# Feed-forward chunks in groups of 3, 6, 6, 7 instead of 4, 6, 6, 6, with the operand splits moved, in a two-layer encoder step

## The reference

```python
def swiglu(h, w_gate, w_up, w_down):
    return (jax.nn.silu(h @ w_gate) * (h @ w_up)) @ w_down
...
    for layer in range(DEPTH):
        x = x + 0.5 * swiglu(rms_norm(x, norm_g[layer, 0]), ffn_w_gate[layer, 0], ffn_w_up[layer, 0], ffn_w_down[layer, 0])
        h = rms_norm(x, norm_g[layer, 1])
        ...
        x = x + 0.5 * swiglu(rms_norm(x, norm_g[layer, 2]), ffn_w_gate[layer, 1], ffn_w_up[layer, 1], ffn_w_down[layer, 1])
    return (rms_norm(x, final_norm_g), ...)
```

## Time and profile before

| | us |
|---|---|
| runs (3) | 1987.78, 1988.15, 1989.62; median 1988.15 |
| the profiled execution, its own time | 1988.24 |
| its span, first to last instruction | 1986.4 |
| PE busy | 1978.6 in 13462 matmuls |
| DVE, ACT, POOL busy | 1418.2, 932.5, 964.0 |
| mean granted TensorE clock | 0.999 of full speed |

### The profile page before, as it was taken

One profiled execution on the slowest core, in us unless ns is written; L12 is line 12 of the kernel. 1 busy time (PEld: TensorE's weight loads), 2 busy tenths in 40 slices (PEclk: granted clock), 3 DMA queues, 4 the chain that ended last, 5 costly groups with the idle time before them and its releaser, 6 DMA issues. The chain is left out here.

```text
span 1986.4 us, 35197 instructions
## 1 busy us (share of the span) xinstructions
PE 1978.6 (100%) x13462; PEld 1957.5 (99%) x13462; DVE 1418.2 (71%) x2263; ACT 932.5 (47%) x1642; POOL 964.0 (49%) x1043
## 2 busy tenths in 40 slices
PE   9999999999999999999999999999999999999998
PEld 8999999999999999999999999999999999999998
DVE  5778687664766667878766668778767866878665
ACT  6354454543434435445455345454545535455443
POOL 2556666632000055676663336666743355666643
PEclk9999999999999999999999999999999999999999
DMA  6232324323222223232432222323332223232412
GB/s 162 74 86 70 101 70 117 101 58 95 66 64 65 56 73 86 77 95 69 117 102 75 64 65 75 96 80 91 102 109 70 67 57 86 77 99 65 122 38 86
DMA packets 312853, 165.28 MB, mean 83 GB/s; under 512 B 15539, under 2 KB 310271, under 8 KB 312688
## 3 DMA queue, kind: packets, MB, share of 16 engines
q1 hardware_dynamic: 307840, 157.31, 28.4%
q0 software_dynamic: 2672, 4.65, 1.0%
q10 hardware_dynamic: 2176, 1.07, 0.2%
HBM read 159.01 MB, written 4.00 MB: 82 GB/s over the span
## 5 line engine op out<-in xcount | busy, mean ns | idle before, releaser
L2401 POOL TENSOR_TENSOR sums<-in_raw,sums 128x256 f32<-128x256 f32 (+1 forms) x416 | 440.1, 1088 | 12.1 <-DVE in_lo L1751 3.9
L2401 POOL TENSOR_TENSOR sums<-in_raw 128x256 f32<-128x256 f32 (+1 forms) x208 | 179.9, 885 | 429.7 <-DVE in_lo L1751 377.4
L895 PE MATMUL psum<-xg_hi,in_lo 128*128 128x320 f32 x1152 | 356.0, 309 | 0.0
L893 PE MATMUL psum<-xg_hi,in_hi 128*128 128x320 f32 x1152 | 355.9, 309 | 0.0
L894 PE MATMUL psum<-xg_lo,in_hi 128*128 128x320 f32 x1152 | 355.9, 309 | 0.0
L1751 DVE TENSOR_TENSOR in_lo<-in_raw,in_hi 128x1024 fp32r<-128x1024 f32 (+1 forms) x208 | 271.9, 1309 | 42.5 <-ACT in_hi L1306 42.2
L893 PE MATMUL psum<-mix_hi,in_hi 128*128 128x320 f32 x864 | 267.0, 309 | 0.0
L894 PE MATMUL psum<-mix_lo,in_hi 128*128 128x320 f32 x864 | 267.0, 309 | 0.0
L895 PE MATMUL psum<-mix_hi,in_lo 128*128 128x320 f32 x864 | 267.0, 309 | 0.0
L1306 ACT ACTIVATE in_hi<-in_raw 128x1024 fp32r<-128x1024 f32 (+1 forms) x208 | 205.0, 991 | 111.7 <-PE psum L895 111.7
L744 PE MATMUL psum<-xg_hi,in_hi 128*128 128x320 f32 x800 | 252.3, 315 | 0.9 <-DVE in_lo L1792 0.6
(11 more groups left out here) (267 smaller groups left out, 4560.9 us busy)
## 6 DMA issues: line engine op xcount, KB each, us to landing
in_raw<-in_ffn_w_gate SPq DMA_DIRECT2D x87, 512.0 KB, 5.2
in_raw<-in_ffn_w_up SPq DMA_DIRECT2D x86, 512.0 KB, 4.0
in_raw<-in_ffn_w_down SPq DMA_DIRECT2D x64, 384.0 KB, 4.0
out_raw<-in_ffn_w_down SPq DMA_DIRECT2D x32, 384.0 KB, 3.5
out_raw<-in_ffn_w_down SPq DMA_DIRECT2D x32, 256.0 KB, 2.9
in_raw<-in_mix_w_in SPq DMA_DIRECT2D x14, 512.0 KB, 4.6
out<-y_nat SPq DMA_DIRECT2D x5, 512.0 KB, 3.1
in_raw<-in_mix_w_in SPq DMA_DIRECT2D x8, 256.0 KB, 4.5
```

The source lines that it names most:

```text
L893: pe.matmul(dst, w_hi[:, k], v_hi, start=k == 0 and slot in (0, 1, 4), stop=False, skip_group_check=True)
L895: end = pe.matmul(dst, w_lo[:, k], v_hi, start=False, stop=k == wide - 1, skip_group_check=True)
L2401: last = pool.tensor_tensor(to[:, part], a[:, part], b[:, part], op)
```

## The change

One chunk per FFN goes from the plain group to the last group, whose outputs then have 7 chunks; `PLAIN` is 3 and `FAST` 19. Around that:

- The plain units are (0,0), (1,0), (0,1), (1,1), (2,0), (2,1) (chunk, half): six instead of eight. The first outputs wait for the third chunk's hidden rows only at that chunk.
- The first outputs have 9 matmuls a unit instead of 12, the last ones 21 instead of 18. Their PSUM banks are turned by one in the last group, since the last step now has the other parity.
- The seven blocks of x are split in another order and place: before T3 and T2 during the plain chunks, B11 and B21, T1, T4 and B22 in the first outputs; now B11, B21 and T1 there, one at a time, and T2, B22, T3 and T4 in the first seven-product step. Parts 3 and 4 of the first step's weights move into that step too.
- The seventh hidden row of the last group has its own place over the weights' sums (`last_hi`, `last_lo`), so its split waits for the last step's weight splits. The last group's upper products use `pair_even`, which lies over the sums of squares `ss`; these are now cleared after that group's hidden rows and not at its first step.

The diff, cut to its core:

```diff
-GROUPS = (4, 6, 6, 6)
+GROUPS = (3, 6, 6, 7)
...
+def ends(fast):
+
+    return fast % FAST in (5, 11, 18)
...
+        last_hi = over("last_hi", [P, TOKENS], arena + 30720, F32R)
+        last_lo = over("last_lo", [P, TOKENS], arena + 33280, F32R)
...
+        def out_bank(g, i, q):
+
+            return 4 + (q + (g == 3)) % out_banks(g, i)
...
-            return (pair_even, pair_odd)[i % 2][:, :] if g in SEVEN else t2a[:, :]
+            return (pair_even, pair_odd)[i % 2][:, :] if g in SEVEN else pair_even[:, :]
...
-        BLOCKS = ["T3", "T2", "B11", "B21", "T1", "T4", "B22"]
+        BLOCKS = ["B11", "B21", "T1", "T2", "B22", "T3", "T4"]
...
                             def before_k(k):
                                 if g == 0 and i == 0 and j == 0 and k == 0:
-                                    pe.wait_ge(hidden_lo, 44 * index + 2 * gk - (2 if half == 0 else 0))
+                                    pe.wait_ge(hidden_lo, 44 * index + 2 * (gk - 1))
+                                if g == 0 and i == 0 and j == 0 and k == gk - 1:
+                                    pe.wait_ge(hidden_lo, 44 * index + 2 * gk - (1 if half == 0 else 0))
...
             def blocks_between(index, phase, i, q):
 
                 if (i, q) == (0, 3):
-                    act.wait_ge(in_mm, IN_UNIT[phase] + 8)
+                    act.wait_ge(in_mm, IN_UNIT[phase] + 2 * PLAIN)
                     block_split("B11")
+                elif (i, q) == (1, 1):
                     block_split("B21")
-                elif (i, q) == (1, 1):
+                elif (i, q) == (1, 3):
+                    act.wait_ge(block_made, 8 * index + MADE["T1"])
                     block_split("T1")
-                elif (i, q) == (1, 3):
-                    act.wait_ge(block_lo, 7 * index + BLOCKS.index("T1") + 1)
-                    block_split("T4")
                 elif (i, q) == (2, 1):
-                    block_split("B22")
+                    fast_high(N_STEPS * index, 1)
                 elif (i, q) == (2, 3):
-                    fast_high(N_STEPS * index, 1)
                     fast_high(N_STEPS * index, 2)
-                elif (i, q) == (3, 1):
-                    fast_high(N_STEPS * index, 3)
-                elif (i, q) == (3, 3):
-                    fast_high(N_STEPS * index, 4)
...
             def hidden_split(i, half, done, src):
                 act.wait_ge(hidden_done, done)
-                act.activation(f_hi[:, i, cols(half)], src, ACT.Copy).then_inc(hidden_hi, 1)
+                if i == SLOTS:
+                    act.wait_ge(fast_split, 4 * N_STEPS * ((done - 1) // 44 + 1))
+                act.activation(hidden_part(f_hi, last_hi, i, half), src, ACT.Copy).then_inc(hidden_hi, 1)
...
+                if s % N_STEPS == 0:
+                    act.wait_ge(block_made, 8 * index + MADE["T2"])
+                    block_split("T2")
+                    fast_high(s, 3)
                 copy(s, fast, 0)
+                if s % N_STEPS == 0:
+                    block_split("B22")
+                    fast_high(s, 4)
...
                 gate_low(fast)
                 if more and not last:
                     fast_high(s + 1, 2)
+                if s % N_STEPS == 0:
+                    block_split("T3")
+                    act.wait_ge(block_made, 8 * index + MADE["T4"])
+                    act.wait_ge(block_lo, 7 * index + BLOCKS.index("T1") + 1)
+                    block_split("T4")
...
                         lower_split(index, g, gk - 1)
+                        dve.wait_ge(hidden_lo, hidden_at(index, g, gk - 1, 1))
+                        for half in range(2):
+                            dve.memset(ss[:, half], 0.0).then_inc(ss_cleared, 1)
```

More of the change, by code:

```diff
@@ L27 @@
 SEVEN = (1, 2)
-assert sum(GROUPS) == FT and max(GROUPS) == SLOTS
+assert sum(GROUPS) == FT and len(PLAIN_UNITS) == 2 * PLAIN
 CHUNK, WINDOW, HD = 64, 128, 64
@@ L137, in weight_slot @@
     return 7 if slot == 5 and s % N_STEPS % 2 else slot
+def ends(fast):
+    return fast % FAST in (5, 11, 18)
 def read_at(fast, which):
-    order = ("low gate", "high up", "high gate") if fast % 6 == 5 else ("low gate", "high gate", "high up")
+    order = ("low gate", "high up", "high gate") if ends(fast) else ("low gate", "high gate", "high up")
     return 3 * fast + order.index(which) + 1
 def copy_at(fast, slot):
-    return 3 * fast + ((0, 2, 4) if fast % 6 == 5 else (0, 4, 2)).index(slot) + 1
+    return 3 * fast + ((0, 2, 4) if ends(fast) else (0, 4, 2)).index(slot) + 1
 def hidden_at(index, g, i, half):
@@ new lines, in ffn @@
+                for q, (f, half) in enumerate(PLAIN_UNITS):
+                    plain = 2 * PLAIN * index + q
+                    if index == 0 and q == 1:
+                        act.wait_ge(in_mm, q + 2)
+                        in_hi_split(q + 1)
+                    if q == 0 and index:
+                        ss_high(NORM[phase])
+                    if q in (0, 2) and index:
+                        rms(NORM[phase], q // 2)
+                    act.wait_ge(gate_scaled, plain + 1)
+                    act.activation(t1[:, q % 2], t1[:, q % 2], ACT.Silu).then_inc(silu_done, 1)
+                    hidden_split(f, half, 44 * index + q + 1, f_t2[q % 2])
+                    if index == 0 and q == 1:
+                        out_hi_split(f_out_hi, 0, 16, GROUPS[0], 0)
+                        out_hi_split(f_out_hi, 1, 16, GROUPS[0], 0)
+                    if q == 2 and index:
+                        act.wait_ge(in_mm, IN_UNIT[phase] + q + 1)
+                        in_hi_split(IN_CHUNK[phase] + q)
@@ new lines, in ffn @@
+                for q, (f, half) in enumerate(PLAIN_UNITS):
+                    b = q % 2
+                    u = 44 * index + q
+                    plain = 2 * PLAIN * index + q
+                    unit = IN_UNIT[phase] + q
+                    bank = in_bank(phase, q)
+                    if q in (0, 2) and index:
+                        norm_factor(m, half)
+                    if q == 2 and not index:
+                        start_factor(1)
+                    dve.wait_ge(in_mm, unit + 1)
+                    wait(dve, hidden_done, u - 1)
+                    dve.tensor_tensor(t1[:, b], psum[:, bank, 0:HALF], rstd[:, half], ALU.mult).then_inc(gate_scaled, 1)
+                    wait(dve, hidden_lo, u - 1)
+                    dve.tensor_tensor(f_t2[b], psum[:, bank + 1, 0:HALF], rstd[:, half], ALU.mult).then_inc(in_read, 1)
+                    if q == 0 and not index:
+                        start_factors(1)
+                    dve.wait_ge(silu_done, plain + 1)
+                    dve.wait_ge(in_read, unit + 1)
+                    dve.tensor_tensor(f_t2[b], f_t2[b], t1[:, b], ALU.mult).then_inc(hidden_done, 1)
+                    hidden_split(f, half, u + 1, f_t2[b])
+                    if index == 0 and q == 3:
+                        out_lo_split(f_out_hi, f_out_lo, 0, 0, GROUPS[0])
+                        out_lo_split(f_out_hi, f_out_lo, 1, 1, GROUPS[0])
+                    if q == 2 and index:
+                        in_lo_split((IN_CHUNK[phase] + q) % 2, SPLIT_CHUNK[phase] + q)
+                    if q == 0 and index > 0:
+                        dve.wait_ge(kv_stored, 16 * 4)
+                        dve.wait_ge(conv_stored, 16 * 2)
+                    if index == 0 and q == 1:
+                        in_lo_split((q + 1) % 2, q + 1)
+                    if q < 4:
+                        normalised(index, m, *((b11_f, "B11", 0, 0), (b21_f, "B21", 1, 0), (b12_f, "B12", 0, 1), (b22_f, "B22", 1, 1))[q])
@@ L2124, in ffn @@
                                     rows_out(rows, turn)
[L2125 removed]
+                            update_x(v + q, 2 * i + b, half, out_bank(g, i, q), 0.5)
                             if half:
```

150 lines of the change are left out of this document (47 added, 103 removed).

## The result

The changed kernel takes 1996.98 us, median of 5 runs (1996.49 to 1998.58), the kernel before 1988.15 (1987.78 to 1989.84): a ratio of 1.0044, with an interval of 1.003 to 1.0057. It is **slower by 0.44%**, 8.8 us, outside the range given (1983.4 to 1992.6) and on the side that had 0.17.

What follows compares the result with a forecast made beforehand. PE bounds the kernel: matmuls times 0.147 us plus its waits. From the profiled 1988.24, gains of 8.66 and new waits of 8.8 (2.2 an FFN) gave 1988.4, as a median 1988.3 us; range 1983.4 to 1992.6.

Steps and rivals of the forecast that it cites:

- the side that had 0.17: Outcome of the whole kernel being slower than no change within 0.2% (1984.3 to 1992.1); chance 0.07 + 0.10 = 0.17.
- G: Second seven-product step: T3's product waits for ACT's copy or DVE's T3 split; 0.5 us, ends 0.2 and 1.3.
- F: First outputs, unit 14: PE waits for DVE's split of the weights of d = 7; 0.5 us, ends 0 and 1.5.
- D: First outputs, unit 4: PE waits for the split weights of d = 2; 0.5 us, ends 0.2 and 1.2.
- Matmuls and last outputs: Gains: 48 fewer matmuls, 7.05 us less; the wait at the last outputs' last chunk gone, 1.24 us less.
- E: First outputs, unit 12: PE waits for DVE's queue to the weights of d = 6; 0.7 us, ends 0 and 1.7.
- DVE keeps up: Rival, first outputs: POOL mostly misses DVE's splits, an FFN costs 0.4 to 1.1 us; say 1982.6 us; chance 0.20.
- ACT is late in the first step: Rival: one more ACT split before T3's product's copy makes that wait 1.7 us; 1993.1 us; chance 0.10.
- The port is held for whole instructions: Rival: every split beside POOL waits a full POOL instruction, 0.96 us; 5.9 an FFN, 2003 us; chance 0.07.
- the 0.96: Upper bound of POOL's extra on a DVE split: half of POOL's 1.93 us for a pair of instructions.
- nothing more: Kernel before, an output-weight split beside POOL that took 0.68 us, counted as an extra of 0.
- w: POOL's mean extra on the six DVE splits that count; 0.35 us used, FFN cost about 6 w + 0.1.

Runs made afterwards that it cites:

- experiment 9: Changed kernel with POOL's T4 difference held until the low split of the output weights of d = 2; 1998.26 us, one run.
- experiment 7: Changed kernel with POOL's sums for the first step's weights held until T1's low split instead of B21's; 1993.63 us, one run.
- experiment 3: Changed kernel with POOL's sums for the second step's weights held until T3's low split; 1991.17 us, one run.
- experiment 1: Changed kernel with ACT's copy in the first step made ahead of T4's high split; 1996.74 us, one run.
- experiment 6: Changed kernel, new groups kept, with block splits where they were before (T3 and T2 in the fifth and sixth plain units); 2020.89 us, 1.0164 of the kernel before.

## Why the prediction was wrong

The mechanism was right: POOL beside DVE's splits makes PE wait, at the four places named. The sizes were not. Of the 9.3 us between 8.8 and 18.1, G is 3.9 and T1's product, which had no term, 2.3; F is 1.2, D 0.8, and the rest stands in FFN 0. The gaps of an FFN sum to 4.3 to 5.2, past the 3.2 that the prediction had set as its sign of being wrong.

- **Matmuls and last outputs**: right. 13414 matmuls, and the wait at the last hidden row is gone in all four FFNs.
- **D**: the chain without POOL was right (0.23; 0.21 measured in experiment 9). POOL's extra was taken as 0.27 and is 1.14 - 0.56 = 0.58. D is 0.8, not 0.5, inside its ends. POOL's work there ended 7.5 after the first matmul (718.81), not 9.2, still later than that split.
- **E**: right, 0.64 for 0.7, by the very splits named (2.04 and 1.00); experiment 7 takes POOL away from them and the wait with it.
- **F**: the extra of part 1 was taken as 0.3 and is 1.75 - 1.18 = 0.57, that of d = 7 as 0.25 and is 0.45. F is 0.76, not 0.5.
- **G is the step that failed.** The prediction put DVE's low split of T3 "near 10.7 too, or 11.2 beside POOL" and took 0.5. Without POOL it ends at 742.38 + 1.49 = 743.87 (experiment 3), and with T3's turn at 743.85 as 10.58, that is 10.60: the chain was right. Beside POOL it ends at 11.91 (746.49 against the turn at 745.16). The extra had been put on T3's split alone, while B22's, part 4's, parts 1 and 2 and T3's stand in one queue and each brings its own: 0.34, 0.55, 0.13, 0.26 and 0.54, 1.8 in all. Of these 1.3 arrive; the others fall into the 0.54 that DVE waits for ACT's high split of part 1 when POOL rests. The wait is 1.5, above G's high end of 1.3.
- **Not priced at all**: T4's split ahead of `gate_high` (0.57). The text asked who stands behind a wait, and looked at ACT's queue in that step but not at DVE's.
- **FFN 0** was counted like the others. There POOL's differences end only at 78.54, 15 us into the first outputs, and its units lose 3.3 instead of 1.7. That the one is the reason for the other was not tried in FFN 0, but experiment 9 made the like in FFN 1: with POOL's last difference put off, units 10 and 12 lost 0.58 and 1.12 there, as against 0.73 and 1.15 here.

By FFN: in FFN 1 to 3, D, F, G and T1's product are 0.3 + 0.26 + 1.0 + 0.57 = 2.1 short, 6.3 in three; FFN 0 is 3.0 short.

The rivals: "DVE keeps up" did not come; DVE was busy 21.2 us in the first outputs of FFN 1, and not some 18. "ACT is late in the first step" has the right product but the wrong engine: experiment 1 moved the copy for nothing. "The port is held for whole instructions" priced 0.96 a split; the extras are 0.58 (d = 2), 0.56 (T1), 0.45 (d = 6 and 7), 0.57 (part 1) and 0.54 (T3), a mean of 0.53. So its point of decision, 0.5, was passed at little over half of its price, and at 6 x 0.53 + 0.1 = 3.3 an FFN the prediction's own sum comes to 1992.7; the rest is G's other splits, T1's product and FFN 0.

No run shows a port, nor what holds a split; the runs show by how much it took longer. That was not a whole POOL instruction but nearly the rest of the one under way. The timeline of POOL instruction by instruction: first in the changed kernel, at the splits of d = 2, d = 3 and T1, then in the kernel before, the pair behind the 0.96.

```profile
715.91 0.87 POOL L2410 TENSOR_TENSOR mix_f<-b_f,mix_f 128x320 f32<-128x320 f32 x1
716.74 1.05 POOL L2424 TENSOR_TENSOR in_raw<-in_raw 128x256 f32<-128x256 f32 x1
724.24 1.09 POOL L2424 TENSOR_TENSOR sums<-in_raw 128x256 f32<-128x256 f32 x1
```

```profile
735.08 0.75 POOL L2401 TENSOR_TENSOR sums<-in_raw 128x256 f32<-128x256 f32 x1 [14.60 <-DVE xg_lo L1757]
735.78 1.22 POOL L2401 TENSOR_TENSOR sums<-in_raw 128x256 f32<-128x256 f32 x1
```

When these three splits begin, the POOL instruction under way has 0.73, 0.27 and 0.69 left, and they take 0.59, 0.14 and 0.55 longer than alone (0.55 and 1.49): each the rest of that instruction less 0.14. In the changed kernel's trace 234 splits of x's blocks and of weights begin with over 0.2 of a POOL TENSOR_TENSOR left and have a width that stands there without POOL too: each takes longer by that rest less 0.13 to 0.15. Where POOL only starts during a split (64 more), the split is longer by 0.01 at most. The other way round, POOL's 1.05 at 716.74 ends 0.60 after the split of d = 2 that it started beside; the 257 POOL instructions of 128x256 that start during such a split end 0.58 to 0.61 after it, and take 0.74 (median of 243) where no split is beside them. The six splits that count (d = 2, T1, d = 6, part 1, d = 7, T3) found 0.58 to 0.73 left and took 0.45 to 0.59 longer; the 0.96 was half of a pair (0.75 and 1.22) whose second instruction started at 735.78, beside the split of 735.72. And the row with "nothing more", which lowered the prediction's w, began with 0.11 of a POOL instruction left (735.83 against 735.72).

The additions to x, which read one operand from PSUM, did not grow: two take 0.88 without POOL (720.08) and beside it (at 734.92 of the earlier trace rows and 735.08 of the earlier trace rows). In the changed kernel 186 of them begin with over 0.2 of a POOL TENSOR_TENSOR left and take 0.47 to 0.49, as do the 152 that have no POOL beside them.

## What to carry to other kernels

Price a contention on every instruction in the queue up to the one that is waited for, not on the last alone, and by what the other engine's instruction takes alone (here POOL's sum of 128x256 took 0.74 alone, and the splits beside it 0.45 to 0.59 longer); and where a queue is filled up, follow it one instruction past the wanted one, to what frees a bank. A split moved into a stage was cheap here only where POOL rested: with the same splits T3's product waited 1.5 us beside POOL and 0.2 without (experiment 3). Units that get shorter shorten the time between a slot's release and its next use; smaller operands can pay for more slots in the same bytes.

## What the runs showed of the hardware that was not expected

In the changed kernel a split of two SBUF operands begun beside POOL took longer by the rest of the POOL instruction under way, less 0.13 to 0.15 us (234 splits), and not by a share of POOL's work: that of d = 2, begun with 0.73 left, took 1.14 us instead of 0.55, and that of d = 3, with 0.27 left, 0.69. POOL's work was longer for the meeting as well. Its sum of four instructions took 6.37 us beside DVE's splits (740.70 in the changed kernel) and 2.85 where they do not meet (746.65 in experiment 3), so it also ended later. And in experiment 6 one PE wait of 5.2 us (726.4 to 731.6) was followed by another 2.5 of loss: the granted clock was 0.50 for the next 5.7 us (731.7 to 737.4), in which 22 matmuls ran that take 22 x 0.147 = 3.2 otherwise.
